# Gathered u and v rows in two rings with two requests, and the requests' new places in GpSimd's queue

## Chip, cores and metric

The kernel runs on one core of one Trainium2 chip. The metric is the device time of one execution in microseconds; that of the kernel before is the median of three runs.

## What is computed

One step of a hybrid encoder layer for 512 prompt tokens and 64 sample tokens, width 1024: an input projection, differential attention beside a gated recurrence, an output projection, cross attention, and then PEER, a layer of 16384 experts of one neuron each. Only PEER matters here. Each token scores two sets of 128 keys for each of 8 heads, takes the best 16 pairs of each head, and so has 128 experts with gates:

```python
e = (take_along_axis(i1, ci // 16) * 128 + take_along_axis(i2, ci % 16))
g = softmax(ts)
ue = u_tab[e]                      # (tokens, 8, 16, 1024)
ve = v_tab[e]
act = gelu(einsum('td,thkd->thk', xt, ue))
out = einsum('thk,thkd->td', g * act, ve)
```

## The kernel before

The five token tiles (four of 128 prompt tokens, one of 64 sample tokens) go through PEER in two ways. Tiles 0 to 2 (384 tokens) are computed **densely**: all 16384 experts for all tokens, in 128 splits of 128 experts, with the gates spread out in a matrix. Tiles 3 and 4 are **gathered**: for every token the rows of u and v of its own experts are fetched from memory by an indirect DMA, 128 rows a step. One row of the table `uv` is u's row and v's row side by side, 8 KB. There are 192 steps: 64 (`EARLY_STEPS`) for the sample tile, whose 128 experts a token are folded on two halves of the partitions, and 128 for tile 3.

A gathered step s is three pieces of work. GpSimd issues the gather into one of four places of `ring`. VectorE's `dot(s)` (L1882) multiplies u's half with the token's row and sums; ScalarE's `coefficient(s)` (L1440, L1446) applies gelu and the gate; VectorE's `accumulate(s)` (L1890) adds v's half times the coefficient to the result. VectorE does dot(s) and then accumulate(s - 2), `LAG = 2`. A gather waits until accumulate of the step whose place it takes is done.

The **split stage** is the loop over the 128 splits n on TensorE. `up(n)` multiplies the split's u weights with the tokens, 24 matmuls (L903), each weight in a high and a low part: `high(n)` is ScalarE's, `low(n)` (L496) GpSimd's, and the weights lie in four places, so that high(n) waits until `up(n - 4)` is done. ScalarE's gelu follows each split. From split 54 on, 48 placing groups g stand between the halves of the splits (`c_tokens`, L927): they multiply 0/1 matrices `hot1`, `hot2` that VectorE makes with three operations a group (L2036, L2038, L2040), to write the dense gates matrix, which goes to memory as `c_scratch`. Group g stands after half split `hot_place(g)`; group 0 after half split 108, group 47 after 250, mostly three apart. `hot_of_step(s) = s * 48 // 64` says behind which group's `hot` operations VectorE does step s, so the groups have one, one and two steps by turns. Two `hot` buffers let VectorE be one group ahead. GpSimd's queue holds low(n) and, between them, the early gathers:

```python
while RING <= issued < EARLY_STEPS and hot_place(hot_of_step(issued - LAG)) // 2 + 4 <= n:
    gather(issued)
    issued += 1
```

ScalarE does the coefficients of group g - 1 when it comes to group g's place, ahead of its copies of the matrix.

The **down stage** is a loop over 128 blocks q: SyncE loads v's weights (`vraw`, 512 KB), the gelu results (`ge`, 192 KB) and every fourth time the gates (`cg`, 768 KB); VectorE multiplies the two (`gf`, L2052); TensorE does 12 matmuls (L951). With each q VectorE does one gathered step of tile 3, in the order gf, dot, accumulate. GpSimd's queue holds nothing but the gathers there. The end is the norm and the store of the result.

Of the kernel before, what the change touches and what calls it, by code (L numbers as in the profile page):

```python
# [24 lines left out]
P = 128  # L25
D = 1024
# [60 lines left out]
def hot_of_step(s):  # L87

    return s * HOTS // EARLY_STEPS
# [83 lines left out]
def encoder_layer(nc: bass.Bass, block, a: dict, o: dict):  # L173
# [139 lines left out]
    r = Region(after_xn)  # L313
    ring = r.put("ring", [P, RING, 2 * D])
    dots = r.put("dots", [P, STEPS])
# [44 lines left out]
    def bank(b, n=BANK, rows=P):  # L360
# [18 lines left out]
    ve_step = S("ve_step")  # L379
    names = """const_in gain_in gain_used memx_in x_in ssq_clear ssq_ready var_ready std_ready xn_ready acth_done  # L380
        out_done lamp_in sp_neg sp_exp sp_one sp_ln lam_sums lam_exp lam_ready conv_done gate_ready m_ready
# [5 lines left out]
        dot_ready acted_ready coef_ready acc_done gates_ready tile3_ready fold_ready folded  # L387
        x2_in y_ready taken_up ss_in iota_copied yg4_copied""".split()
    (const_in, gain_in, gain_used, memx_in, x_in, ssq_clear, ssq_ready, var_ready, std_ready, xn_ready, acth_done,
     out_done, lamp_in, sp_neg, sp_exp, sp_one, sp_ln, lam_sums, lam_exp, lam_ready, conv_done, gate_ready, m_ready,  # L390
# [5 lines left out]
     dot_ready, acted_ready, coef_ready, acc_done, gates_ready, tile3_ready, fold_ready, folded,  # L396
     x2_in, y_ready, taken_up, ss_in, iota_copied, yg4_copied) = [S(name) for name in names]
    ck_in = [S(f"ck_in{j}") for j in range(2)]
# [10 lines left out]
    v_in = [S(f"v_in{j}") for j in range(V_RING)]  # L409
    gather_in = [S(f"gather_in{j}") for j in range(RING)]  # L410
    ss_store = [S(f"ss_store{j}") for j in range(2)]
# [60 lines left out]
    @block.gpsimd  # L472
    def _(pool):
        with pool.Fori(0, PRE_CHUNKS // 2) as i:
            for s in range(4):
                w = raw[:, s % 2, :]
                hi = wH[:, s].rearrange("p k n -> p (k n)")
                lo = wL[:, s].rearrange("p k n -> p (k n)")

                pool.wait_ge(raw_in[s % 2], i * 32 + 16 * (s // 2 + 1))  # L480
                pool.wait_ge(w_free, i * 4 + (s // 2 * 2 + 2))

                pool.sem_inc(taken_up, 1)
                cuts = (slice(0, PIECE // 2), slice(PIECE // 2, PIECE))
                for cut in cuts:
                    pool.tensor_scalar(hi[:, cut], w[:, cut], 1.0, 1.0, ALU.mult, ALU.mult).then_inc(high_done, 1)  # L486
                for c, cut in enumerate(cuts):

                    pool.wait_ge(high_done, i * 8 + (2 * s + c + 1))
                    pool.tensor_tensor(lo[:, cut], w[:, cut], hi[:, cut].bitcast(F32), ALU.subtract)\  # L490
                        .then_inc(w_ready, 1)

        def low(n):
            pool.wait_ge(hi_done, n + 1)
            u = n % U_RING
            pool.tensor_tensor(uL[:, u].rearrange("p k n -> p (k n)"), uraw[:, u, :],  # L496
                               uH[:, u].rearrange("p k n -> p (k n)").bitcast(F32), ALU.subtract).then_inc(lo_done, 1)

        def gather(s):
            if s >= RING:  # L500
                pool.wait_ge(acc_done, s - RING + 1)
            if s == STEPS4:
                pool.wait_ge(tile3_ready, 1)
            pool.indirect_dma_start(out=ring[:, s % RING, :], out_offset=None, in_=a["uv"],  # L504
                                    in_offset=bass.IndirectOffsetOnAxis(ap=place_of[:, s:s + 1], axis=0))\
                .then_inc(gather_in[s % RING], 16)

        def two_halves(out, of):

            for half in range(2):  # L510
                pool.dma_start(out[half * NS_TOK:(half + 1) * NS_TOK, 0:STEPS4],
                               of[0:NS_TOK, half * STEPS4:(half + 1) * STEPS4]).then_inc(picks_in, 16)

        issued = 0
        for n in range(NKEYS):
            low(n)
            if n == PICKS_AT:
                pool.wait_ge(picks_ready, 1)
                two_halves(place_of, eu)
            if n == PICKS_AT + 1:  # L520

                pool.wait_ge(ssb_ready, N_PQ * TILES)
                pool.wait_ge(picks_in, 32)
                for s in range(RING):
                    gather(s)
                issued = RING
            if n == GATES_AT:
                pool.wait_ge(gates_ready, 1)
                two_halves(gates_of, chosen[:, DENSE, 2, :])
            while RING <= issued < EARLY_STEPS and hot_place(hot_of_step(issued - LAG)) // 2 + 4 <= n:  # L530
                gather(issued)
                issued += 1
        for s in range(issued, STEPS):
            gather(s)

# [434 lines left out]
    def _(act):  # L970
# [443 lines left out]
        def copy_choices():  # L1414

            act.wait_ge(chT_ready, DENSE)
            act.wait_ge(iota_in, 16)
            act.activation(iota_ps, iota[:, :], ACT.Copy).then_inc(iota_copied, 1)
            for i in range(DENSE):
                act.activation(chosenT[:, :, i * P:(i + 1) * P],  # L1420
                               ps[:, i * BANK:i * BANK + 2 * P].rearrange("p (s t) -> p s t", s=2),
                               ACT.Copy).then_inc(chT_copied, 1)
# [77 lines left out]
    def _(ve):  # L1500
# [375 lines left out]
        def dot(s):  # L1876
            ve.wait_ge(gather_in[s % RING], 16 * (s // RING + 1))
            if s == 0:
                ve.wait_ge(rows_in, 16)
            x_at = 0 if s < STEPS4 else 1  # L1880
            row = ring[:, s % RING, 0:D]
            ve.scalar_tensor_tensor(row, row, 1.0, xn[:, x_at, :], ALU.mult, ALU.mult, accum_out=dots[:, s:s + 1])\  # L1882
              .then_inc(dot_ready, 1)

        def accumulate(s):
            ve.wait_ge(coef_ready, s + 1)
            if s:
                ve.wait_ge(acc_done, s)
            y = yg4 if s < STEPS4 else yg[:, 1, :]
            ve.scalar_tensor_tensor(y, ring[:, s % RING, D:2 * D], coef[:, s:s + 1], y, ALU.mult, ALU.add)\  # L1890
              .then_inc(acc_done, 1)
# [133 lines left out]
        ve.wait_ge(chT_copied, DENSE)  # L2025
        ve.wait_ge(iota_copied, 1)
        for g in range(HOTS):
# [61 lines left out]
        for j, i in enumerate(LAST):  # L2089
# [12 lines left out]

INPUTS = ["wts", "wu", "wv", "uv", "ident", "x", "mem", "gains", "par", "lamp", "gsub", "ropec", "ropes", "ropen", "mask", "ckT", "cv",
          "cmkT", "cmv", "keysT", "iota"]
# [4 lines left out]
def layout(p):  # L2109
# [28 lines left out]
    for at, name in ((PAR_CB, "conv_b"), (PAR_BA, "rg_ba"), (PAR_BX, "rg_bx")):  # L2138
# [18 lines left out]
    arrays = {  # L2157
        "wts": wts, "wu": wu, "wv": wv, "uv": np.concatenate([u, v_rows], axis=1), "ident": np.eye(P, dtype=f32),
        "x": np.concatenate([p["x_prompt"][0], p["x_sample"][0]]), "mem": p["mem_prompt"][0],
# [32 lines left out]
```

## Time and profile before

| | |
|---|---|
| median of 3 runs | 2619.72 us (2613.31 to 2626.7) |
| profiled execution, its own time | 2624.7 us |
| its span | 2622.9 us |
| granted TensorE clock, mean | 0.92 |
| TensorE / VectorE / ScalarE / GpSimd busy | 89% / 57% / 25% / 35% |
| moved | 541.94 MB, 207 GB/s |
| 192 gathers, 1 MB each | median 8.2 us from issue to landing |
| share of the gathers in the chain that ended last | 20% |

A busy share is an average over stages with different limits. "PEld" rows are TensorE's weight loads, which run beside its matmuls; a matmul's end is modelled. The granted clock is a share of full speed, and a DMA share of 1 means that all 16 engines have packets under way.

### The profile page before, as it was taken

How to read it: one execution, taken by the hardware profiler on the slowest of the kernel's cores; microseconds unless marked ns; L12 is line 12 of the kernel's file. 1: busy time of each engine (PE TensorE's matmuls, PEld its weight loads, DVE VectorE, ACT ScalarE, POOL GpSimd, SP SyncE). 2: the span in 40 equal slices, each digit the busy share in tenths (PEclk: the TensorE clock that was granted, in tenths of full speed). 3: DMA queues.
4: the chain of work that ended last, by engine and by line, in shares of the span. 5: the costliest groups of instructions: out<-in, count | busy, mean ns of one | idle time of the engine just before them, and what ended most of it. 6: DMA issues, size and time to landing. Idle time of an engine off the chain costs nothing.

```text
span 2622.9 us, 29598 instructions
## 1 busy us (share of the span) xinstructions
PE 2339.0 (89%) x11005; PEld 1786.3 (68%) x11005; DVE 1487.4 (57%) x2697; ACT 667.5 (25%) x1421; POOL 927.9 (35%) x552
## 2 busy tenths in 40 slices
PE   6799999899789999999977777777789999999996
PEld 6699977655468879999977777777734444344442
DVE  2376654444632334999985656665445555555555
ACT  2244420123322312333433333333200000000001
POOL 8454554400014244266644444444311111111110
PEclk9799999855799999999988888888899999999998
DMA  6323233200133121366547677777899999999995
GB/s 233 107 97 109 94 127 113 89 16 16 48 94 137 49 95 64 107 230 177 171 125 289 244 267 272 271 279 262 301 357 367 360 358 360 340 362 355 353 365 207
DMA packets 192546, 541.94 MB, mean 207 GB/s; under 512 B 17057, under 2 KB 116194, under 8 KB 158882
## 3 DMA queue, kind: packets, MB, share of 16 engines
q1 hardware_dynamic: 113024, 243.30, 28.1%
q0 software_dynamic: 27776, 201.40, 20.1%
q10 hardware_dynamic: 51618, 95.52, 10.0%
q8 instruction: 81, 1.33, 0.2%
q14 instruction: 47, 0.39, 0.0%
HBM read 472.18 MB, written 67.67 MB: 206 GB/s over the span
## 4 chain that ended last, share of the span: by engine, by line
PE 44%; DVE 23%; DMA 22%; issue 5%; ACT 3%; POOL 3%; ACTq 1%; SPq 0%; DVEq 0%; POOLq 0%
DMA ring<-uv,place_of 20%; PE ps L578 16%; PE ps L951 7%; PE ps L903 5%; PE ps L695 4%; PE ps L927 3%; PE ps L728 3%; DVE yg L1890 2%; PE ps L557 2%; PE ps L778 2%; POOL uL L496 1%; PE ps L732 1%; DVE chosen L1965 1%; POOL wL L490 1%; DVE pickf L1964 1%
## 5 line engine op out<-in xcount | busy, mean ns | idle before, releaser
L951 PE MATMUL ps<-vraw,gf 128*128 128x512 f32 x1536 | 675.7, 601 | 42.1 <-DVE gf L2052 31.1
L951 PEld LDWEIGHTS ps<-vraw,gf 128*128 128x128 f32 x1536 | 292.7, 192 | 424.7 <-issue 367.3
L1882 DVE SCALAR_TENSOR_TENSOR ring<-ring,xn 128x1024 f32<-128x1024 f32 x192 | 249.1, 1298 | 498.1 <-DMA ring<-uv,place_of 498.0
L496 POOL TENSOR_TENSOR uL<-uraw,uH 128x1024 fp32r<-128x1024 f32 x128 | 328.6, 2571 | 344.0 <-ACT uH L1391 343.7
L504 POOL DMA_INDIRECT ring<-uv,place_of x192 | 195.4, 1018 | 657.2 <-DVE yg L1890 573.2
L903 PE MATMUL ps<-actH,uH 128*128 128x384 f32 x1024 | 351.4, 343 | 2.7 <-POOL uL L496 2.0
L486 POOL TENSOR_SCALAR wH<-raw 128x1024 fp32r<-128x1024 f32 x112 | 120.9, 1099 | 646.1 <-PE ps L578 493.3
L903 PE MATMUL ps<-actL,uH 128*128 128x384 f32 x1024 | 345.7, 338 | 0.0
L903 PE MATMUL ps<-actH,uL 128*128 128x384 f32 x1024 | 345.1, 337 | 0.0
L578 PE MATMUL ps<-actH,wH 128*128 128x288 f32 (+1 forms) x960 | 287.1, 299 | 7.0 <-DVE actL L1552 7.0
L578 PE MATMUL ps<-actH,wL 128*128 128x288 f32 (+1 forms) x960 | 285.1, 297 | 0.0
L578 PE MATMUL ps<-actL,wH 128*128 128x288 f32 (+1 forms) x960 | 284.9, 297 | 0.0
L490 POOL TENSOR_TENSOR wL<-raw,wH 128x1024 fp32r<-128x1024 f32 x112 | 283.8, 2557 | 0.0
L927 PE MATMUL ps<-hot,hot 128*128 128x128 f32 x768 | 120.9, 323 | 119.6 <-DVE hot L2040 119.6
L1440 ACT ACTIVATE acted<-dots 128x1 f32<-128x1 f32 x192 | 38.4, 200 | 680.0 <-DVE ring L1882 669.4
L927 PEld LDWEIGHTS ps<-hot,hot 128*128 128x128 f32 x768 | 115.4, 235 | 126.0 <-DVE hot L2040 126.0
L903 PEld LDWEIGHTS ps<-actH,uH 128*128 128x128 f32 x1024 | 195.9, 191 | 3.2 <-ACT ge L1406 2.3
L903 PEld LDWEIGHTS ps<-actL,uH 128*128 128x128 f32 x1024 | 195.7, 191 | 0.0
L903 PEld LDWEIGHTS ps<-actH,uL 128*128 128x128 f32 x1024 | 194.9, 190 | 0.0
L578 PEld LDWEIGHTS ps<-actH,wH 128*128 128x128 f32 x960 | 183.6, 191 | 8.2 <-DVE actL L1552 7.9
L578 PEld LDWEIGHTS ps<-actL,wH 128*128 128x128 f32 x960 | 183.4, 191 | 0.3
L578 PEld LDWEIGHTS ps<-actH,wL 128*128 128x128 f32 x960 | 183.3, 191 | 0.0
(290 smaller groups left out, 3311.4 us busy)
## 6 DMA issues: line engine op xcount, KB each, us to landing
uraw<-wu SPq DMA_DIRECT2D x128, 512.0 KB, 4.0
vraw<-wv SPq DMA_DIRECT2D x128, 512.0 KB, 6.9
raw<-wts SPq DMA_DIRECT2D x56, 1024.0 KB, 4.9
ge_scratch<-ge ACTq DMA_DIRECT2D x128, 192.0 KB, 4.2
c_scratch<-cst ACTq DMA_DIRECT2D x12, 2048.0 KB, 9.2
cg<-c_scratch SPq DMA_DIRECT2D x32, 768.0 KB, 9.8
ge<-ge_scratch SPq DMA_DIRECT2D x128, 192.0 KB, 7.2
xres<-x ACTq DMA_DIRECT2D x2, 2048.0 KB, 12.1
```

Of the source, the lines that this page charges most:

```text
L486: pool.tensor_scalar(hi[:, cut], w[:, cut], 1.0, 1.0, ALU.mult, ALU.mult).then_inc(high_done, 1)
L490: pool.tensor_tensor(lo[:, cut], w[:, cut], hi[:, cut].bitcast(F32), ALU.subtract)\
L496: pool.tensor_tensor(uL[:, u].rearrange("p k n -> p (k n)"), uraw[:, u, :], uH[:, u].rearrange("p k n -> p (k n)").bitcast(F32), ALU.subtr ...
L504: pool.indirect_dma_start(out=ring[:, s % RING, :], out_offset=None, in_=a["uv"], in_offset=bass.IndirectOffsetOnAxis(ap=place_of[:, s:s + ...
L557: mm = pe.matmul(out, lhs, rhs, start=t == 0, stop=t == len(terms) - 1)
L578: mm = pe.matmul(cols(b), lhs, rhs, start=k == 0 and t == 0, stop=k == KT - 1 and t == 2)
L695: mm = pe.matmul(cols(b), lhs, rhs, start=k == 0 and t == 0, stop=k == KT - 1 and t == 2)
L728: mm = pe.matmul(bank(b, n), qT[half, h, t], kT[half, h, 0:n], start=True, stop=False)
L903: mm = pe.matmul(bank(b, TD), lhs, rhs, start=k == 0 and w == 0, stop=k == KT - 1 and w == 2)
L927: mm = pe.matmul(ps[:, at:at + P], hot1[:, g % 2, 4 * half + t, :], hot2[:, g % 2, 4 * half + t, :], start=True, stop=True)
L951: mm = pe.matmul(bank(2 * i + half), gf[:, q % GF_RING, i * P:(i + 1) * P], vraw[:, q % V_RING, half * CHUNK:(half + 1) * CHUNK], start=q ...
L1882: ve.scalar_tensor_tensor(row, row, 1.0, xn[:, x_at, :], ALU.mult, ALU.mult, accum_out=dots[:, s:s + 1])\
```

## The change

The ring becomes two, `ring_u` and `ring_v`, of the same size together, and the table `uv` becomes two tables; each step has two requests of 128 rows of 4 KB. The request for u(s) waits for dot(s - 4), that for v(s) for accumulate(s - 4). In GpSimd's queue both stand two splits further forward (`+ 2` for `+ 4`), and u's goes by the group of step s - 4 in place of s - 2. Behind the splits, u runs up to three steps ahead of v. One wait of VectorE (`iota_copied`) goes, which stood behind a wait for later work of the same engine, and an unused semaphore.

```diff
-    ring = r.put("ring", [P, RING, 2 * D])
+    ring_u = r.put("ring_u", [P, RING, D])
+    ring_v = r.put("ring_v", [P, RING, D])
...
-        def gather(s):
+        def gather_u(s):
+
+            if s == STEPS4:
+                pool.wait_ge(tile3_ready, 1)
+            if s >= RING:
+                pool.wait_ge(dot_ready, s - RING + 1)
+            pool.indirect_dma_start(out=ring_u[:, s % RING, :], out_offset=None, in_=a["u_rows"],
+                                    in_offset=bass.IndirectOffsetOnAxis(ap=place_of[:, s:s + 1], axis=0))\
+                .then_inc(urow_in[s % RING], 16)
+
+        def gather_v(s):
+
             if s >= RING:
                 pool.wait_ge(acc_done, s - RING + 1)
-            if s == STEPS4:
-                pool.wait_ge(tile3_ready, 1)
-            pool.indirect_dma_start(out=ring[:, s % RING, :], out_offset=None, in_=a["uv"],
+            pool.indirect_dma_start(out=ring_v[:, s % RING, :], out_offset=None, in_=a["v_rows"],
                                     in_offset=bass.IndirectOffsetOnAxis(ap=place_of[:, s:s + 1], axis=0))\
-                .then_inc(gather_in[s % RING], 16)
+                .then_inc(vrow_in[s % RING], 16)
...
                 for s in range(RING):
-                    gather(s)
-                issued = RING
+                    gather_u(s)
+                    gather_v(s)
+                u_next = v_next = RING
...
-            while RING <= issued < EARLY_STEPS and hot_place(hot_of_step(issued - LAG)) // 2 + 4 <= n:
-                gather(issued)
-                issued += 1
-        for s in range(issued, STEPS):
-            gather(s)
+            while RING <= u_next < EARLY_STEPS and hot_place(hot_of_step(u_next - RING)) // 2 + 2 <= n:
+                gather_u(u_next)
+                u_next += 1
+            while RING <= v_next < EARLY_STEPS and hot_place(hot_of_step(v_next - LAG)) // 2 + 2 <= n:
+                gather_v(v_next)
+                v_next += 1
+        while v_next < STEPS:
+            if u_next < min(STEPS, v_next + LAG + 1):
+                gather_u(u_next)
+                u_next += 1
+            else:
+                gather_v(v_next)
+                v_next += 1
...
-            ve.wait_ge(gather_in[s % RING], 16 * (s // RING + 1))
+            ve.wait_ge(urow_in[s % RING], 16 * (s // RING + 1))
...
             ve.wait_ge(coef_ready, s + 1)
+            ve.wait_ge(vrow_in[s % RING], 16 * (s // RING + 1))
...
-        ve.wait_ge(iota_copied, 1)
```

GpSimd's queue around the first early requests, before: `uL` rows are low(n), and the row with x43 ends at low(59); `ring` rows are gathers, the first of them that of step 4.

```order
L496 TENSOR_TENSOR uL<-uraw,uH 128x1024 [waits hi_done] x43
L504 DMA ring<-uv,place_of 128x2048 [waits acc_done]
L496 TENSOR_TENSOR uL<-uraw,uH 128x1024 [waits hi_done] x2
L504 DMA ring<-uv,place_of 128x2048 [waits acc_done]
L496 TENSOR_TENSOR uL<-uraw,uH 128x1024 [waits hi_done]
L504 DMA ring<-uv,place_of 128x2048 [waits acc_done] x2
L496 TENSOR_TENSOR uL<-uraw,uH 128x1024 [waits hi_done] x2
L504 DMA ring<-uv,place_of 128x2048 [waits acc_done]
```

And after the change; the row with x40 ends at low(56).

```order
L498 TENSOR_TENSOR uL<-uraw,uH 128x1024 [waits hi_done] x40
L507 DMA ring_u<-u_rows,place_of 128x1024 [waits dot_ready] x2
L498 TENSOR_TENSOR uL<-uraw,uH 128x1024 [waits hi_done]
L507 DMA ring_u<-u_rows,place_of 128x1024 [waits dot_ready]
L515 DMA ring_v<-v_rows,place_of 128x1024 [waits acc_done]
L498 TENSOR_TENSOR uL<-uraw,uH 128x1024 [waits hi_done] x2
L507 DMA ring_u<-u_rows,place_of 128x1024 [waits dot_ready]
L515 DMA ring_v<-v_rows,place_of 128x1024 [waits acc_done]
L498 TENSOR_TENSOR uL<-uraw,uH 128x1024 [waits hi_done]
```

The first request of the split stage moved from behind low(59) to behind low(56) and is now two, for u of steps 4 and 5; v of step 4 follows behind low(57), and each step takes two requests between the low parts.

The same queue where the splits end, before: the gather of step 64 and the 127 behind it.

```order
L496 TENSOR_TENSOR uL<-uraw,uH 128x1024 [waits hi_done] x2
L504 DMA ring<-uv,place_of 128x2048 [waits acc_done] x2
L496 TENSOR_TENSOR uL<-uraw,uH 128x1024 [waits hi_done]
L504 DMA ring<-uv,place_of 128x2048 [waits tile3_ready,acc_done]
L504 DMA ring<-uv,place_of 128x2048 [waits acc_done] x127
```

After:

```order
L498 TENSOR_TENSOR uL<-uraw,uH 128x1024 [waits hi_done] x2
L515 DMA ring_v<-v_rows,place_of 128x1024 [waits acc_done] x2
L498 TENSOR_TENSOR uL<-uraw,uH 128x1024 [waits hi_done] x3
L507 DMA ring_u<-u_rows,place_of 128x1024 [waits dot_ready,tile3_ready]
L507 DMA ring_u<-u_rows,place_of 128x1024 [waits dot_ready] x2
L515 DMA ring_v<-v_rows,place_of 128x1024 [waits acc_done]
L507 DMA ring_u<-u_rows,place_of 128x1024 [waits dot_ready]
L515 DMA ring_v<-v_rows,place_of 128x1024 [waits acc_done]
L507 DMA ring_u<-u_rows,place_of 128x1024 [waits dot_ready]
```

Where one kind of request stood, u and v now alternate, u three steps ahead, each with a wait of its own.

## Rows read from the trace of the kernel before

**Rows 1.** Busy time by stage: us, then each engine, PEclk, DMA share, GB/s
```profile
1348.00:1874.00 526.00, 420.45 (x2484) 414.36 (x2485) 331.23 (x336) 191.57 (x366) 239.77 (x133) 0.89 0.71 259
1874.00:1893.00 19.00, 8.64 (x50) 8.32 (x49) 2.99 (x4) 3.49 (x8) 1.74 (x2) 0.86 1.02 382
1893.00:2600.00 707.00, 675.22 (x1536) 292.70 (x1536) 370.58 (x510) 64.14 (x256) 124.28 (x124) 0.98 0.98 352
```

**Rows 2.** Waits of the split stage: us in total, times, longest
```profile
DVE ring L1882 <- DMA ring<-uv,place_of: 187.9, 34, 12.3
...
PEld ps L927 <- DVE hot L2040: 126.0, 20, 14.9
...
DVE ps L1890 <- ACT coef L1446: 4.4, 1, 4.4
```

**Rows 3.** Chain that ended last, from 1400: start, us, what
```profile
1404.62 1.78 PE ps L927 x16
1406.40 6.24 PE ps L903 x36
...
1435.57 2.05 PE ps L927 x16
...
1459.09 3.78 PE ps L927 x16
```

**Rows 4.** All placing weight loads of L927: count, first and last start
```profile
L927 PEld LDWEIGHTS ps<-hot,hot x768: 186/192/338, 1348.5 to 1871.9; 128*128 128x128 f32 x192
```

**Rows 5.** VectorE in order of time, one group of one step
```profile
1389.83 1.22 DVE L2036 TENSOR_TENSOR hot<-ps,chosenT 128x1024 f32<-128x1024 f32 x1
...
1393.35 1.25 DVE L1882 SCALAR_TENSOR_TENSOR ring<-ring,xn 128x1024 f32<-128x1024 f32 x1
...
1395.72 1.21 DVE L2036 TENSOR_TENSOR hot<-ps,chosenT 128x1024 f32<-128x1024 f32 x1
```

**Rows 6.** Gathers of the split stage: issue on GpSimd, landing
```profile
L504 POOL DMA_INDIRECT ring<-uv,place_of x63: 932/952/1878, 1364.8 to 1873.9; - x63
...
DMA to landing us min/median/max: 5.4/8.2/14.4
```

**Rows 7.** ScalarE in order of time, gelu and the coefficients behind it
```profile
1420.71 0.49 ACT L1406 ACTIVATE ge<-ps 128x384 f32<-128x384 f32 x1 [1.86 <-PE ps L903]
...
1421.61 0.20 ACT L1440 ACTIVATE acted<-dots 128x1 f32<-128x1 f32 x1 [0.40 <-ACT ge L1406]
1421.84 0.29 ACT L1446 ACTIVATE coef<-acted,gates_of 128x1 f32<-128x1 f32 x1
1422.04 0.19 ACT L1440 ACTIVATE acted<-dots 128x1 f32<-128x1 f32 x1
1422.26 0.29 ACT L1446 ACTIVATE coef<-acted,gates_of 128x1 f32<-128x1 f32 x1
```

**Rows 8.** Waits of the down stage
```profile
DVE ring L1882 <- DMA ring<-uv,place_of: 310.1, 117, 7.4
...
PE ps L951 <- DVE gf L2052: 31.1, 19, 6.8
```

**Rows 9.** Chain that ended last: the down stage's longest stretch without a wait
```profile
2533.31 67.22 PE ps L951 x156
```

**Rows 10.** DMA queues of the down stage: packets, MB, share of 16 engines
```profile
q0 software_dynamic: 17881, 130.11, 48.5%
q1 hardware_dynamic: 84625, 115.85, 47.8%
```

**Rows 11.** DMA at 1150 to 1340: queue, and issues with median landing
```profile
q1 hardware_dynamic: 6531, 23.76, 44.4%
...
uraw<-wu SPq DMA_DIRECT2D x45, 512.0 KB, 3.9
```

**Rows 12.** The same at 100 to 400
```profile
q1 hardware_dynamic: 2880, 20.97, 21.0%
...
raw<-wts SPq DMA_DIRECT2D x20, 1024.0 KB, 4.8
```

More of the change, by code:

```diff
@@ L379, in encoder_layer @@
     ve_step = S("ve_step")
-    names = """const_in gain_in gain_used memx_in x_in ssq_clear ssq_ready var_ready std_ready xn_ready acth_done
+    names = """const_in gain_in memx_in x_in ssq_clear ssq_ready var_ready std_ready xn_ready acth_done
         out_done lamp_in sp_neg sp_exp sp_one sp_ln lam_sums lam_exp lam_ready conv_done gate_ready m_ready
@@ L387, in encoder_layer @@
         dot_ready acted_ready coef_ready acc_done gates_ready tile3_ready fold_ready folded
-        x2_in y_ready taken_up ss_in iota_copied yg4_copied""".split()
-    (const_in, gain_in, gain_used, memx_in, x_in, ssq_clear, ssq_ready, var_ready, std_ready, xn_ready, acth_done,
+        x2_in y_ready taken_up ss_in yg4_copied""".split()
+    (const_in, gain_in, memx_in, x_in, ssq_clear, ssq_ready, var_ready, std_ready, xn_ready, acth_done,
      out_done, lamp_in, sp_neg, sp_exp, sp_one, sp_ln, lam_sums, lam_exp, lam_ready, conv_done, gate_ready, m_ready,
@@ L396, in encoder_layer @@
      dot_ready, acted_ready, coef_ready, acc_done, gates_ready, tile3_ready, fold_ready, folded,
-     x2_in, y_ready, taken_up, ss_in, iota_copied, yg4_copied) = [S(name) for name in names]
+     x2_in, y_ready, taken_up, ss_in, yg4_copied) = [S(name) for name in names]
     ck_in = [S(f"ck_in{j}") for j in range(2)]
@@ L409, in encoder_layer @@
     v_in = [S(f"v_in{j}") for j in range(V_RING)]
-    gather_in = [S(f"gather_in{j}") for j in range(RING)]
+    urow_in = [S(f"urow_in{j}") for j in range(RING)]
+    vrow_in = [S(f"vrow_in{j}") for j in range(RING)]
     ss_store = [S(f"ss_store{j}") for j in range(2)]
@@ L512, in two_halves @@
                                of[0:NS_TOK, half * STEPS4:(half + 1) * STEPS4]).then_inc(picks_in, 16)
-        issued = 0
+        u_next = v_next = 0
         for n in range(NKEYS):
@@ L1417, in copy_choices @@
             act.wait_ge(iota_in, 16)
-            act.activation(iota_ps, iota[:, :], ACT.Copy).then_inc(iota_copied, 1)
+            act.activation(iota_ps, iota[:, :], ACT.Copy)
             for i in range(DENSE):
@@ L1880, in dot @@
             x_at = 0 if s < STEPS4 else 1
-            row = ring[:, s % RING, 0:D]
+            row = ring_u[:, s % RING, :]
             ve.scalar_tensor_tensor(row, row, 1.0, xn[:, x_at, :], ALU.mult, ALU.mult, accum_out=dots[:, s:s + 1])\
@@ L1889, in accumulate @@
             y = yg4 if s < STEPS4 else yg[:, 1, :]
-            ve.scalar_tensor_tensor(y, ring[:, s % RING, D:2 * D], coef[:, s:s + 1], y, ALU.mult, ALU.add)\
+            ve.scalar_tensor_tensor(y, ring_v[:, s % RING, :], coef[:, s:s + 1], y, ALU.mult, ALU.add)\
               .then_inc(acc_done, 1)
@@ L2100, in _ @@
                                     ALU.mult, ALU.mult).then_inc(y_ready, 1)
-INPUTS = ["wts", "wu", "wv", "uv", "ident", "x", "mem", "gains", "par", "lamp", "gsub", "ropec", "ropes", "ropen", "mask", "ckT", "cv",
+INPUTS = ["wts", "wu", "wv", "u_rows", "v_rows", "ident", "x", "mem", "gains", "par", "lamp", "gsub", "ropec", "ropes", "ropen", "mask", "ckT", "cv",
           "cmkT", "cmv", "keysT", "iota"]
@@ L2157, in layout @@
     arrays = {
-        "wts": wts, "wu": wu, "wv": wv, "uv": np.concatenate([u, v_rows], axis=1), "ident": np.eye(P, dtype=f32),
+        "wts": wts, "wu": wu, "wv": wv, "u_rows": u, "v_rows": v_rows, "ident": np.eye(P, dtype=f32),
         "x": np.concatenate([p["x_prompt"][0], p["x_sample"][0]]), "mem": p["mem_prompt"][0],
```

## Prediction

> **What bounds the kernel now.** I read the busy shares by stage first [rows 1]. Two stretches matter to this change. The **split stage**, where the placing matmuls of L927 stand between those of L903, takes 526.0 us, and TensorE works 420.45 of them at a granted clock of 0.89; the **down stage** takes 707.0 us with TensorE busy for 675.22 at 0.98. The transfers differ more: share 0.71 and 259 GB/s against 0.98 and 352 GB/s.
>
> Next the waits of the split stage [rows 2]. TensorE's weight loads wait 126.0 us, 20 times, for `hot` of VectorE; the first of these (14.9) lies before 1348.5 almost wholly, so 19 waits and 111 us lie inside. VectorE for its part waits 187.9 us for the gather, 34 times. The chain [rows 3] shows what a stall costs beyond itself: 16 placing matmuls take 1.78 us between other work, 2.05 or 3.78 behind a stall (the clock was down to its 1.2 GHz level there), and 36 of L903 take 6.24.
>
> TensorE's own work follows from that. From the first to the last placing group [rows 4] lie 142 half splits, 71 splits of 24 matmuls at 6.24/36 = 0.173 us, 4.16 each, together 295.4; 48 groups at 1.78 add 85.4. That is 380.8 us of 526.0. The excess is 145: 111 of waits and some 34 of slow clock behind them.
>
> In the down stage VectorE waits even longer for the gather, 310.1 us, but TensorE only 31.1 for `gf` [rows 8]. A stretch without waits runs 156 matmuls in 67.22 us [rows 9], 5.17 for the 12 of one q, 662 us for 128; the stage takes 707, or 5.52 a q. Its transfers are at the limit by the share. So the gather's lateness binds the first stage, and the amount moved binds the second.
>
> **The change part by part.** *Earlier requests, split stage.* Let P be the split in which the placing group of step s-2 lies. The old request for step s stands behind low(P+4); low(n) can't run before TensorE begins split n-3, so the request leaves at P+1 plus a split's fraction for ScalarE and GpSimd, say P+1.8. A split with its part of the placing takes 380.8/71 = 5.36 us. The `hot` that stands behind dot s is due at P+4.5 at the latest, 2.7 splits or 14.5 us later. In that time there must pass 8.2 from issue to landing (5.4 to 14.4) [rows 6], 2.4 for dot and accumulation (twice that in a group of two steps) and 3.5 for three `hot` operations [rows 5]: 14.1 to 16.5, so up to 2 us late at the median landing and up to 8 at the longest. Measured are 111/48 = 2.3 a group.
>
> The new request for u of step s stands two splits further forward and goes by the group of step s-4, 2.3 splits earlier again: 4.3 splits, 23 us sooner. Its place is free at dot s-4, three groups (24 us) before it is used. v gains two splits (11 us) and is needed only two steps later, at the accumulation. Against a landing of 8.2, 14.4 at worst, both are in time. The cover for this is the ring's 24 us; it is gone if landings pass some 20.
>
> *What is late next.* VectorE's work in three groups is 3 x 3.52 + 4 x 2.37 = 20.0 us [rows 5] against TensorE's 3 x 8.02 = 24.1. Accumulation s-2 can need a coefficient of the group before, which ScalarE computes behind the gelu: gelu at 1420.71, second coefficient done at 1422.55 [rows 7], so 1.9 us after TensorE could begin its placing. Then 1.2 for the accumulation and 3.5 for `hot`: 6.6 of 8.02, in time by 1.4. GpSimd issues two requests a step in place of one, 64 x 0.95 us more [rows 6]; it waits in queue order for dot_ready and acc_done, and behind it stands low(P+3). That wait ends about when TensorE does split P, low(P+3) is due three splits later, so 16 us cover it. The transfers' own work is 0.71 x 526 = 373 us [rows 1], just under the 381 of TensorE: little room, and bursts will be felt. I leave 25 us for them, half a microsecond for each of 48 groups: less than a quarter of the 111 of today, as the landings that hurt are the longest only. Bounds: 0 (floor 381) and 60 (434, below). Stage: 406, gain **120**.
>
> *Earlier requests, down stage.* In flight now are at most two gathers of 1 MB, later up to four u and four v of half that. The amount is the same. At share 0.98 there are 14 us (2% of 707) that a fuller queue can win.
>
> *Twice the packets.* A gathered row of 8 KB becomes two of 4 KB. In the down stage [rows 10] q0 spends 0.485 x 707 x 16 / 17881 = 0.307 us on a packet of 7276 bytes, q1 0.478 x 707 x 16 / 84625 = 0.064 on one of 1369. A line through both gives 0.0076 us a packet beside its bytes: 128 more packets on 16 engines are 0.06 us a step, 8 us in the down stage and 4 in the split stage (hidden there if TensorE is the bound). I take the line, since it is from this stage and at this load. Bounds: nothing, and the rows of streams without gathers beside them [rows 11, 12]: 20 requests of 1 MB held the engines for 0.210 x 300 / 20 = 3.15 us each, 45 of half that size for 0.444 x 190 / 45 = 1.88, so two halves cost 0.6 more than the whole. Gain 14 less 8, less a little for a fuller queue that SyncE's loads must share: I take **0** for the down stage.
>
> The Trainium skill, "DMA: Bandwidth & Descriptors", section "Anatomy of one DMA", gives 2.0 us plus bytes/436e3 for one software request. By that (an estimate) two halves cost 2.0 us more than one whole; laid end to end over 128 steps, this would be 256 us. The trace bears out the latency (half the bytes land in 3.9 us, the whole in 4.8 [rows 11, 12]) but not the adding up: gathers that land in 8.2 us come every 5.5.
>
> *The rest*: the dropped wait for iota_copied stands behind one for the same engine's later work; nothing.
>
> **Sum.** 2624.7 - 120 - 0 = 2504.7 by the profiled execution, which lies 5 us above the median of the runs: **2500**.
>
> **The rivals.**
> *A. The down stage gains too* (0.12). If share 0.98 hides latency and not capacity, more requests in flight let it run to TensorE's 662 plus some 13 of start: 675, 32 less, 2468. For it: the 19 us between the stages moved 382 GB/s. Against: 352/0.98 = 359 GB/s, and the split stage has 259/0.71 = 365 per full share [rows 1], so both show the same ceiling. The skill's same page, section "Where 436 GB/s comes from", puts a core's half of the memory at some 358 and measured 425 with the neighbour idle; the rows agree with the first.
> *B. Half requests hold the engines longer* (0.13, and 0.04 for its far end). With x us more a step the down stage takes 128x more, and the split stage 373 + 64x + 6 once that passes 406. At q1's rate of today, 115.85/(0.478 x 707) = 343 GB/s against q0's 379 [rows 10], x is 0.29: 2500 + 37 + 0 = 2537, with some disturbance of the first stage 2543. At the 0.6 of the lone streams: 418 and +77, 2589. **The other side:** at the uraw rate of 23.76 MB/(0.444 x 190) = 281 GB/s [rows 11], x is 0.98: split stage 440 (the upper bound above), down stage +125, so 2500 + 34 + 125 = 2659, slower. It decides at x = 0.76, a gather rate of 297 GB/s. Against it: those streams were alone and paid their start each time.
> *C. ScalarE's coefficient takes the gather's place* (0.08). If the 1.4 us of room are short by 3 in two groups of three, 96 us come on the floor: 477, a gain of 49, 2571. For it: VectorE waited for it once already, 4.4 us [rows 2].
> *D. Nothing moves* (0.03): landings under a share near 1 grow with what is in flight, and VectorE waits as long as before.
>
> **How the numbers follow.** The likeliest (0.60) reaches from 2480 to 2525 (residue 5 to 50 us). Range 2450 to 2570: it takes in A, B up to 0.4 us a step, and stops at C. Some 13 us (0.5%) is what a measurement can tell here. Faster by more: 0.60 + 0.12 + 0.13 + 0.08 = 0.93; D is the same, 0.03; slower 0.04.
>
> **What would show it.** In the split stage: weight loads' wait for `hot` under 35 us, VectorE's for gathers under 50 (that for coef may rise to 30), a clock of 0.95 or more, a share of 0.9; length 400 to 430. In the down stage: 695 to 715 at a share of 0.98 or more, u and v landing in 8 us and more as before. A down stage under 685 speaks for A, over 735 for B; `hot` late with gathers in time and coef as releaser for C. The forecast fails most likely in the down stage, where one tenth of a microsecond in a step is 13 us.

## The result, and the profile after

The changed kernel takes 2473.96 us (median of four runs, 2465.09 to 2476.26) against 2621.14 for the kernel before (2613.31 to 2626.7): a ratio of 0.943, with a 95% interval of 0.940 to 0.947. The forecast of 2500 was 26 us too high: within its range of 2450 to 2570, but below the 2480 to 2525 of its likeliest case. The profiled execution took 2465.09 us, with a span of 2463.3, and is the fastest of the four.

By stage, the rows that answer to [rows 1]:

```profile
1347.00:1746.00 399.00, 389.61 (x2483) 384.68 (x2484) 392.88 (x336) 191.18 (x366) 287.95 (x196) 0.99 0.93 342
1746.00:1764.00 18.00, 8.70 (x51) 8.38 (x49) 2.25 (x3) 3.00 (x6) 1.53 (x2) 0.84 1.01 377
1764.00:2441.00 677.00, 664.72 (x1537) 293.00 (x1538) 368.31 (x512) 65.99 (x259) 311.47 (x250) 0.99 1.00 369
```

The split stage went from 526 to 399 us, the down stage from 707 to 677. These are 127 and 30 of the 159.6 us between the two profiled executions (2624.7 to 2465.1); the other 2.6 are in the stretches before, between and behind them. TensorE's clock is 0.99 in both, and the share of the transfers 0.93 and 1.00, with 342 and 369 GB/s against 259 and 352.

The waits of the split stage (us in total, times, longest), beside [rows 2]:

```profile
POOL ring_u L507 <- DVE ring_u L1902: 92.7, 59, 12.6
...
PEld ps L947 <- DVE hot L2060: 24.1, 17, 10.3
...
POOL ring_v L515 <- DVE ps L1911: 20.4, 45, 4.4
...
DVE ps L1911 <- ACT coef L1466: 4.1, 1, 4.1
```

TensorE's wait for `hot` fell from 126.0 to 24.1, VectorE's for the gather from 187.9 to nothing that is listed. The new place of waiting is GpSimd, 92.7 us for dots. And VectorE is busy for 392.88 of the 399 us, more than any other engine. The row of its dots in the split stage, by tile (shortest, median, longest in ns):

```profile
L1902 DVE SCALAR_TENSOR_TENSOR ring_u<-ring_u,xn x64: 1209/1364/5093, 1347.3 to 1742.1; 128x1024 f32<-128x1024 f32 x64
```

In the down stage:

```profile
L1902 DVE SCALAR_TENSOR_TENSOR ring_u<-ring_u,xn x128: 1209/1218/1283, 1763.5 to 2425.9; 128x1024 f32<-128x1024 f32 x128
```

A dot takes 1.22 us, but in the split stage the longest takes 5.09. What stands beside the long ones is seen in order of time. VectorE from 1377 to 1403 (start, us):

```profile
1376.01 1.28 DVE L1911 SCALAR_TENSOR_TENSOR ps<-ring_v,coef,ps 128x1024 f32<-128x1024 f32 x1
...
1380.71 4.90 DVE L1902 SCALAR_TENSOR_TENSOR ring_u<-ring_u,xn 128x1024 f32<-128x1024 f32 x1
...
1385.55 1.28 DVE L1911 SCALAR_TENSOR_TENSOR ps<-ring_v,coef,ps 128x1024 f32<-128x1024 f32 x1
...
1390.25 1.35 DVE L1902 SCALAR_TENSOR_TENSOR ring_u<-ring_u,xn 128x1024 f32<-128x1024 f32 x1
...
1396.24 3.71 DVE L1902 SCALAR_TENSOR_TENSOR ring_u<-ring_u,xn 128x1024 f32<-128x1024 f32 x1
...
1401.07 1.21 DVE L1902 SCALAR_TENSOR_TENSOR ring_u<-ring_u,xn 128x1024 f32<-128x1024 f32 x1
```

GpSimd in the same stretch, where L498 is the low part and the brackets are its idle time and what ended it:

```profile
1377.59 0.94 POOL L515 DMA_INDIRECT ring_v<-v_rows,place_of  x1 [0.30 <-DVE ps L1911]
1378.83 0.94 POOL L515 DMA_INDIRECT ring_v<-v_rows,place_of  x1 [0.30 <-issue]
1379.79 4.74 POOL L498 TENSOR_TENSOR uL<-uraw,uH 128x1024 fp32r<-128x1024 f32 x2
1385.89 0.95 POOL L507 DMA_INDIRECT ring_u<-u_rows,place_of  x1 [1.37 <-DVE ring_u L1902]
1387.15 0.94 POOL L515 DMA_INDIRECT ring_v<-v_rows,place_of  x1 [0.30 <-DVE ps L1911]
1388.11 2.40 POOL L498 TENSOR_TENSOR uL<-uraw,uH 128x1024 fp32r<-128x1024 f32 x1
```

The dot of 1380.71 starts inside the two low parts that GpSimd runs from 1379.79 for 4.74 us, and ends 1.1 us behind them, at 1385.6. The one of 1390.25 meets only the last 0.3 us of a low part and takes 1.35; the one of 1401.07 meets none and takes 1.21. So it is in the whole stage: 46 of the 64 dots take over 1.3 us, each of them begins inside a low part and ends 1.08 to 1.10 us behind the last of the low parts that run there without a pause; none of the other 18 begins inside one. The accumulations of this stage, which have one of their inputs in PSUM (`ps`), take 1.29 us at most.

In the down stage the wait of VectorE for the gather [rows 8] is gone too, and it waits for the loads instead:

```profile
DVE gf L2072 <- DMA ge<-ge_scratch: 299.5, 76, 25.5
...
PE ps L971 <- DVE gf L2072: 11.7, 2, 11.2
PE ps L971 <- DMA vraw<-wv: 9.8, 1, 9.8
```

Those 299.5 us cost little: TensorE lost 21.5 us to both of its waits, `gf` and the first load. Before, it lost 31.1 to `gf` [rows 8] and 10.7 to the first load:

```profile
PE ps L951 <- DMA vraw<-wv: 10.7, 1, 10.7
```

That is 20 of the stage's 30 us; the rest is TensorE's own work, 664.72 us at a granted clock of 0.99 for 675.22 at 0.98. The DMA queues (packets, MB, share), beside [rows 10]:

```profile
q0 software_dynamic: 36000, 131.09, 49.9%
q1 hardware_dynamic: 84481, 115.47, 48.7%
```

q0 has twice the packets, as it should, and took 0.499 of the stage for 131.09 MB: 388 GB/s, more than the 379 of before (130.11 MB in 0.485 of 707 us, [rows 10]).

### The profile page after: what moved, and what is told of

Its sections match the earlier page's. It is cut to its first block, busy times and chain, and to the rows that moved or that the text cites. A ratio compares the mean times of both kernels' runs of the same rounds, so it can differ in the third digit from the quotient of the medians.

```text
span 2463.3 us, 29790 instructions
## 1 busy us (share of the span) xinstructions
PE 2297.0 (93%) x11005; PEld 1757.1 (71%) x11005; DVE 1544.5 (63%) x2697; ACT 666.8 (27%) x1421; POOL 1166.9 (47%) x744
## 3 DMA queue, kind: packets, MB, share of 16 engines
q10 hardware_dynamic: 51618, 95.52, 10.7%
## 4 chain that ended last, share of the span: by engine, by line
PE 56%; DVE 31%; issue 5%; DMA 3%; ACT 2%; SPq 2%; POOL 1%; ACTq 0%; POOLq 0%; DVEq 0%
PE ps L971 24%; PE ps L598 17%; DVE ring_u L1902 5%; PE ps L715 5%; DVE ps L1911 3%; PE ps L748 3%; DVE hot L2058 2%; DVE hot L2056 2%; DMA ge<-ge_scratch 2%; PE ps L577 2%; PE ps L798 2%; PE ps L752 1%; SPq L447 1%; DVE pickp L1982 1%; DVE chosen L1986 1%
## 5 line engine op out<-in xcount | busy, mean ns | idle before, releaser
L971 PE MATMUL ps<-vraw,gf 128*128 128x512 f32 x1536 | 664.7, 595 | 21.6 <-DVE gf L2072 11.7
L507 POOL DMA_INDIRECT ring_u<-u_rows,place_of x192 | 235.9, 1229 | 411.6 <-DVE ring_u L1902 391.8
L498 POOL TENSOR_TENSOR uL<-uraw,uH 128x1024 fp32r<-128x1024 f32 x128 | 323.4, 2539 | 116.0 <-ACT uH L1411 114.9
L1902 DVE SCALAR_TENSOR_TENSOR ring_u<-ring_u,xn 128x1024 f32<-128x1024 f32 x192 | 312.8, 1629 | 0.0
L2072 DVE TENSOR_TENSOR gf<-ge,cg 128x384 f32<-128x384 f32 x128 | 71.8, 561 | 305.4 <-DMA ge<-ge_scratch 305.0
L515 POOL DMA_INDIRECT ring_v<-v_rows,place_of x192 | 203.9, 1062 | 71.4 <-issue 45.6
```

The costliest lines, as they stand in the source:

```text
L507: pool.indirect_dma_start(out=ring_u[:, s % RING, :], out_offset=None, in_=a["u_rows"], in_offset=bass.IndirectOffsetOnAxis(ap=place_of[:, ...
L515: pool.indirect_dma_start(out=ring_v[:, s % RING, :], out_offset=None, in_=a["v_rows"], in_offset=bass.IndirectOffsetOnAxis(ap=place_of[:, ...
L971: mm = pe.matmul(bank(2 * i + half), gf[:, q % GF_RING, i * P:(i + 1) * P], vraw[:, q % V_RING, half * CHUNK:(half + 1) * CHUNK], start=q ...
```

## Experiments

Stage lengths come from each trace, the split stage from the first placing group to the last, the down stage from the first of its matmuls to the last; a whole is the median of the runs, with its ratio to the kernel before, run on the same chip beside it. "+4" and "+2" are the splits that the queue's condition adds; "s-4" and "s-2" say by which step's group u's request goes. "Paired": behind the splits u runs no steps ahead of v.

| kernel | u, v requests | place in the splits | split stage | down stage | whole | ratio |
|---|---|---|---|---|---|---|
| before | one | +4 | 526 | 707 | 2621.1 | 1 |
| e1_two_requests | two, dot waits for both | +4 | 534 | 747 | 2672.6 | 1.020 (1.017 to 1.023) |
| e1c_u_alone | two, dot waits for u | +4 | 495 | 673 | 2561.4 | 0.978 (0.975 to 0.981) |
| e3_old_places | as changed | +4, u by s-2 | 499 | 680 | 2577.1 | 0.984 (0.980 to 0.987) |
| e2_forward_only | one | +2 | 426 | 703 | 2526.4 | 0.966 (0.962 to 0.969) |
| e4_no_lead_down | as changed, paired behind the splits | +2 | 399 | 676 | 2469.2 | 0.940 (0.937 to 0.944) |
| after_again | as changed | +2 | 399 | 678 | 2470.3 | 0.943 (0.940 to 0.945) |
| e10_plus3 | as changed | +3 | 403 | 676 | 2474.2 | 0.944 (0.942 to 0.947) |
| e12_plus4 | as changed | +4, u by s-4 | 390 | 678 | 2464.6 | 0.940 (0.938 to 0.943) |
| e13_plus4_paired | as e12, paired | +4, u by s-4 | 388 | 674 | 2463.4 | 0.940 (0.937 to 0.942) |
| e5_low_halves | as changed, low part in halves | +2 | 406 | 681 | 2467.5 | 0.940 (0.937 to 0.943) |
| e8_low_eighth | as changed, an eighth of the low part | +2 | 386 | 679 | 2455.0, one run | |
| e9_low_memset | as e8, with a memset | +2 | 386 | 680 | 2456.1, one run | |

A stage's length is from one trace a kernel. Eight traces have the changed kernel's code in the down stage; they give 676 to 681 us for it.

Theory and rivals at the start: what counts is the *lead* of a request before its use; against it, that *half requests* run better or worse by themselves, and that the *place* freed at dot is the point.

**Two requests and nothing else.** The request for u waits for acc_done as v's does, both stand at the old place, one behind the other, and the dot waits for both:

```diff
             ve.wait_ge(urow_in[s % RING], 16 * (s // RING + 1))
+            ve.wait_ge(vrow_in[s % RING], 16 * (s // RING + 1))
```

> Two rings and two half requests a step, but with everything else as before: both wait for accumulate(s-4), stand at the old places, and dot waits for u and v. Theory 'lead' (what counts is how long before its use a request is issued): split stage 526 us and down stage 707 us as in the kernel before, plus at most 12 us for the doubled packets, so 2620 to 2635 us. Rival 'size' (half requests by themselves let the transfers run faster): down stage 690 or less, whole 2605 or less. Rival 'half requests hold the engines longer' (0.6 us a step): 2690 or more.

It was slower by 2.0% (1.7 to 2.3), outside all three expectations: 2672.6 us lies between "lead" and "half requests hold the engines longer". Its stages (columns as in [rows 1]):

```profile
1354.00:1888.00 534.00, 425.80 (x2486) 419.65 (x2487) 352.07 (x336) 191.60 (x367) 297.54 (x194) 0.88 0.72 256
1907.00:2654.00 747.00, 683.12 (x1536) 291.20 (x1536) 368.59 (x509) 63.17 (x254) 243.16 (x248) 0.98 0.94 333
```

Its gathers in the down stage, with the median from issue to landing, and their queue:

```profile
ring_u<-u_rows,place_of POOLq DMA_INDIRECT x124, 6.8
ring_v<-v_rows,place_of POOLq DMA_INDIRECT x124, 7.5
...
q0 software_dynamic: 35781, 130.26, 47.9%
```

The down stage took 40 us more, 0.31 a step. The DMA engines were not held: the share is 0.94, lower than before. The loss is in the round from a freed place to the next arrival, which takes two steps, as dot(s) uses what was requested behind accumulate(s - 4). v's half lands 7.5 us after the start of its issue, which is 1.3 us after the start of u's (1.01 for u's issue, 0.30 to the next): together 8.8 against 8.2 for the whole before. With 0.3 us from the freed place to the issue and 2.4 for dot and accumulation the round is, by this estimate from medians, 10.9 us before and 11.5 here; measured are 11.05 (707/64) and 11.67 (747/64). Half the request lands only 0.7 us sooner than the whole, and the second issue costs more than that.

**Dot waits for u alone.** The same without that added wait.

> As the kernel with two requests and nothing else, but dot waits for u alone, v only at the accumulation. Lead: half the data stand ahead of dot, so it starts some 1 to 2 us sooner; split stage 470 to 510, down stage 690 to 700, whole 2550 to 2595 us. Rival 'place' (u's place freed at dot is the point): no gain without it, 2615 us or more.

The whole takes 111 us less than the kernel above. By the two traces it is 118, 74 of it in the down stage and 39 in the split stage. Its stages:

```profile
1351.00:1846.00 495.00, 418.55 (x2485) 411.70 (x2486) 343.55 (x336) 191.00 (x366) 298.75 (x194) 0.92 0.77 275
1865.00:2538.00 673.00, 665.83 (x1538) 293.87 (x1538) 372.54 (x510) 65.61 (x257) 246.02 (x248) 0.99 1.01 370
```

Its waits in the down stage, TensorE's and VectorE's:

```profile
DVE ring_u L1901 <- DMA ring_u<-u_rows,place_of: 243.8, 113, 5.2
...
PE ps L970 <- DMA vraw<-wv: 10.3, 1, 10.3
...
PE ps L970 <- DVE gf L2071: 7.2, 1, 7.2
```

So the down stage's whole gain (673 us, the shortest of all) is there once v may come two steps later: VectorE still waits 243.8 us for u, TensorE next to nothing for VectorE. The whole (2561.4) and the split stage (495) came within the forecast of "lead"; the down stage is 17 us under its 690 to 700. The "place" theory fell: u's place was still held until the accumulation.

**One request, two splits forward.** In the kernel before, `hot_place(...) // 2 + 2 <= n` for `+ 4`.

> The kernel before with its one request moved two splits further forward (+2 for +4) and nothing else. Lead: the request then waits mostly for accumulate(s-4) itself, 8.2 us of landing against two steps of about 12 us, so most of the split stage's waits go: 430 to 460 us; the down stage has no such places and stays at 707; whole 2535 to 2560 us. Rival 'place': the request can't leave before accumulate(s-4), so the stage stays above 500 us and the whole above 2590.

100 of the split stage's 127 us come from this line alone; the down stage, where the line has no part, stayed at 703. Both the stage (426) and the whole (2526.4) came out a little below the forecast of "lead", far below that of "place". The waits of its split stage:

```profile
POOL ring L504 <- DVE ps L1890: 202.4, 61, 25.8
...
DVE ring L1882 <- DMA ring<-uv,place_of: 53.8, 20, 7.7
PEld ps L927 <- DVE hot L2040: 44.0, 14, 14.8
```

GpSimd now waits 202.4 us with the request in hand, so what its request waits for is the place of the ring, free only at the accumulation; VectorE still waits 53.8 us for the gather, and the stage is 27 us longer than in the changed kernel. That the place is why is argued from these waits.

**Rings as changed, old places.**

```diff
+            while RING <= u_next < EARLY_STEPS and hot_place(hot_of_step(u_next - LAG)) // 2 + 4 <= n:
+                gather_u(u_next)
+                gather_v(u_next)
```

> The changed kernel with both requests at the old places of the split stage (+4, group of step s-2), the down stage as changed. Lead: down stage 677 us as in the changed kernel; split stage between before and after, 450 to 500, because u needs half the data; whole 2520 to 2570 us. If the places were of no account, 2474 us.

Both of its stages came out as said, 499 and 680; the whole, 2577.1, is 7 us above the 2570 of the forecast. Against e1c_u_alone it shows what u's freed place and, in the down stage, three steps of lead bring: no gain, in either stage (499 against 495, 680 against 673).

**No lead of u behind the splits.** `u_next < min(STEPS, v_next + 1)` for `v_next + LAG + 1`.

> The changed kernel, but behind the splits u no longer runs up to three steps ahead of v: GpSimd issues u(s), v(s), u(s+1). The kernel in which only dot's wait for v had gone already had a down stage of 673 us by its trace, so if two steps more for v are what counts, the down stage is 670 to 680 here too and the whole 2465 to 2480 us. If the early u (its place free at dot) carries part of the down stage's gain, 685 or more and 2485 or more.

676 us and 2469.2, within the first of the two expectations, and no slower than the changed kernel. VectorE waits 62.8 us for u here, which costs TensorE nothing that shows.

**The low part in halves.** Two tensor_tensor of 512 columns for one of 1024.

> The changed kernel with GpSimd's low part of each split done in two operations of 512 columns. Theory 'lock' (a dot, which reads two tensors of SBUF, stands still while a GpSimd operation that reads SBUF runs): if dot can step in between two GpSimd operations, the dots' 1.6 us mean of the split stage falls to 1.5 and less and the stage from 398 to 385 to 392 us, whole 2460 to 2468. If GpSimd's next operation takes the port before dot does (as two low parts in a row did, 4.9 us), no change, 2470 to 2478.

2467.5 us (0.940, 0.937 to 0.943), the split stage 406 by its trace, and the dots' sum in one same window of 393 us 163.07 against 156.29 in the changed kernel. A dot didn't come in between two GpSimd operations: one that began at 1374.77 took 5.17 us, through four halves that ran from 1373.83 to 1378.84. The whole fell where the first theory had it (2460 to 2468), and yet the dots, and the split stage of 406 us, are as the second has them. So this kernel is inconclusive on the time, and clear on the order of access.

**An eighth of the low part, and a memset for the rest.** From split 54 on; the low weights left out are part of the computation.

```diff
-            pool.tensor_tensor(uL[:, u].rearrange("p k n -> p (k n)"), uraw[:, u, :],
+            cut = P if n >= HOT_AT else D
+            pool.tensor_tensor(uL[:, u].rearrange("p k n -> p (k n)")[:, 0:cut], uraw[:, u, 0:cut],
```

> The changed kernel, from split 54 on with an eighth of the low part (128 of 1024 columns; the rest of the low weights is left out, so the time is that of less work on GpSimd). Lock: no dot over 1.7 us, the dots' sum in the split stage falls from 157 us to 80, and the stage goes down to TensorE's 381 to 386 us, whole about 2450. If the dots are long because of the transfers' writes into SBUF, they stay long and the stage stays at 398.

> As the one before, with the left-out 896 columns filled by a GpSimd memset, which writes SBUF and reads none. If the dots' standing still comes from GpSimd's reading, they stay at 1.2 us and the stage at 381 to 386; if any GpSimd operation on SBUF does it, dots of 2 us and more are there again and the stage is 388 or more.

They ran at 2455 and 2456 us (one run each), with the split stage at 386 in both. The dots of the first:

```profile
L1904 DVE SCALAR_TENSOR_TENSOR ring_u<-ring_u,xn x64: 1215/1218/1254, 1348.0 to 1728.3; 128x1024 f32<-128x1024 f32 x64
```

And of the second, with the memset:

```profile
L1906 DVE SCALAR_TENSOR_TENSOR ring_u<-ring_u,xn x64: 1215/1219/1348, 1347.1 to 1727.5; 128x1024 f32<-128x1024 f32 x64
```

GpSimd's memset in the second, 71 times 0.86 us in that stage:

```profile
L500 POOL MEMSET uL<- 128x896 f32 x71 | 61.1, 861 | 18.3 <-ACT uH L1415 18.2
```

With most of GpSimd's reading gone no dot takes over 1.35 us, and the stage is 13 us shorter; the transfers, which moved 355 GB/s there, are not the cause. That GpSimd's writes are not the cause either rests on less than the 61 us of memsets: only ten of the 64 dots met one, and nine of these memsets began inside the dot. Each of the ten dots took 1.22 us, and each of these memsets 0.85 or 0.86: neither waited for the other. So the long dots come from GpSimd's operations that read SBUF. The Trainium skill states this: "SBUF — State Buffer", section "Who interferes with whom", says that a VectorE instruction with two SBUF inputs contends with a GpSimd instruction that reads SBUF and not with one that only writes it, and that the second to start waits for the whole of the first. Dot reads `ring_u` and `xn`; these rows agree, 1.22 us without and up to 5.09 with. They show one thing more: the dot of 1380.71 let both of two low parts pass that followed each other, and those of e5_low_halves up to four.

**Other places.** Both one split later (`+ 3`); or `+ 4` with u by the group of s - 4; and this with the paired order.

> The changed kernel with both requests one split later (+3 for +2). Theory 'ring of waits' (GpSimd, at the request, waits for the dot just done, then does its low parts, and these hold up the next dot): one split later the dot waited for is long done, the low parts come when ScalarE releases them, fewer of them meet a dot, and the dots' sum in the split stage falls from 157 us to 100 to 130; stage 385 to 393, whole 2458 to 2468. Rival 'lead': one split less of lead (5.4 us) brings waits for the gather back, stage 405 or more, whole 2480 or more.

> The changed kernel with both at +4 as in the kernel before, but u still by the group of step s-4 (so 2.3 splits ahead of the old place), v by that of step s-2 (the old place). v is needed only at the accumulation two steps later, so its old place is early enough. Ring of waits: stage 383 to 390 us, whole 2455 to 2465. Lead: if v's two splits were needed, waits for ring_v appear, stage 410 or more.

> The one before with the down stage's order u(s), v(s) in place of u three steps ahead: down stage 673 to 677 by the two kernels that had it, so 0 to 5 us less than the one before, the best of all: 2452 to 2464 us.

And the changed kernel beside them:

> The changed kernel once more, beside the three that follow: 2465 to 2480 us, split stage 398 us, down stage 677.

`+ 3` was a miss: 403 us and 2474.2. The dots' sum fell to 144 us only, not to 100 to 130, and TensorE's weight loads waited 29.7 us for `hot`, more than in the changed kernel. `+ 4` with u by s - 4 came out as said (2464.63, 2463.99 to 2467.77). Paired it has the lowest median, 2463.42 us (2462.82 to 2465.67), by less than the runs differ among themselves; both are under the 2470.32 (2468.41 to 2476.03) of the changed kernel run beside them. The paired kernel's waits in the split stage:

```profile
DVE ps L1911 <- ACT coef L1466: 28.4, 15, 4.5
...
PEld ps L947 <- DVE hot L2060: 15.6, 4, 12.3
```

GpSimd waits for dots for 0.3 us in all there, dots take 116 us in place of 157, and the coefficient (28.4 us) is VectorE's longest wait.

## Why the prediction was right

**The whole.** The direction and the range held. The medians are 147 us apart where 120 were forecast, and 2474 lies below the likeliest case (0.60) and beside the 2468 of rival A, which had 0.12. So it was the width of the range, drawn to take in A, that made room for the result, and not its central sum. The sign that the prediction had named for A, a down stage under 685 us, came true too.

**What bounds the stages.** That the gather's lateness bound the split stage is shown by one moved line that took 100 us (e2_forward_only). The floor of 381 us held within 5: with short dots the stage takes 386.

**Split stage: 406 forecast, 399 measured, gain 120 against 127.** The size was nearly right, in part by luck: the 25 us of residue were set down to bursts of transfers that make landings late, and no wait for a gather is listed, with landings up to 14.0. (Its upper bound stands as 434 in one place and as 440 in another; 381 and 60 are 441.) Most of the 18 us over the floor are dots held up by low parts, as 13 of them went when the low parts were cut (e8_low_eighth): the dots take 157.5 us in this stage where 64 x 1.22 = 78 would do, and VectorE, which I had at 20.0 of 24.1 us for three groups, is busy for 392.88/16 = 24.6. The chain that ended last goes through it (start, us), a round of three groups from one of these rows to the next, 76.2 us for three:

```profile
1376.08 1.20 DVE ps L1911
...
1402.29 1.20 DVE ps L1911
...
1426.12 1.20 DVE ps L1911
...
1452.29 1.20 DVE ps L1911
```

In the trace before, eight of the 64 dots already took 2.1 to 3.4 us, and I took the one dot of [rows 5] without looking at the longest of its kind in that stage:

```profile
L1882 DVE SCALAR_TENSOR_TENSOR ring<-ring,xn x64: 1217/1226/3423, 1348.4 to 1869.8; 128x1024 f32<-128x1024 f32 x64
```

**GpSimd's waits in queue order** were costed at nothing, with 16 us of cover. Low parts were in time, as said. What I missed is that these waits tie GpSimd to VectorE: it leaves its wait when a dot is done, issues its requests, and starts the low parts just as the next dot comes. With the requests placed later the tie is gone, and the stage is 388 to 390 us. That the tie is the cause is argued, from the waits (92.7 us for dots against 0.9 and 0.3), the order in time and a count. The 71 low parts of 2.4 us fill 43% of the changed kernel's stage, so by chance, an estimate, some 27 of 64 dots would begin inside one. The dots over 1.3 us are 46 there, and 27 and 24 in e12_plus4 and e13_plus4_paired. `+ 3`, which still has 54.2 us of the wait and 39 such dots, gained nothing.

**Down stage: 0 forecast, 30 measured.** This step failed: "At share 0.98 there are 14 us (2% of 707) that a fuller queue can win." With it fell the reading against rival A that 359 and 365 GB/s per full share are one ceiling, and the agreement that the prediction saw there with the lower of the two rates it quoted. The stage moved 369 at 1.00 and 370 at 1.01. A share near 1 said that the engines always had packets under way, not that they could move no more. What bound the stage, by the estimate beside e1_two_requests, was the round of the ring, two steps long: the requests waited for accumulate(s - 4), and the dot for the whole row. Rival A gave 675 us for this stage; 677 were measured. Its mechanism needs a correction: not the many requests in flight but that v may come two steps later, since e1_two_requests and e1c_u_alone issue their requests by the same rule, and differ by 74 us in the one wait for v. TensorE is now the bound there, with 664.72 of 677 us busy, so no run shows how much more the engines could move.

**Twice the packets.** The line through the two queues gave 0.06 us a step. Two requests by themselves cost 0.31. The sum of the round in e1_two_requests puts that down to the second issue on GpSimd, with no run that has the issue alone. The packets' own time is small: by q0's rows two packets of 4 KB take 0.320 us in e1_two_requests and 0.300 in the changed kernel, where one of 8 KB took 0.307. So the term was put at the wrong resource. In the changed kernel it is hidden, as VectorE has no wait for a gather there, and rival B didn't come: q0's rate rose.

**The coefficient (rival C)** is a wait of VectorE of 4.1 us in the changed kernel, of 30.0 and 28.4 in e12_plus4 and e13_plus4_paired, and of 66.3 in e8_low_eighth. It costs almost nothing: TensorE's weight loads wait 3.3 us for `hot` in e13_plus4_paired beyond the one wait of 12.3, and in e8_low_eighth, where the stage is the shortest, once, for 6.4 us. The 96 us of rival C didn't come; the 1.4 us of room itself was not measured.

**The sum.** 127 + 30 + 2.6 = 159.6 against 120, so 2465 for the profiled execution in place of 2505. That execution lies 9 us under the median of its four, while the one before lay 4 above that of its own; 12 us of the 159.6 come from there, and the medians give 147.

## What to carry to other kernels

Split a transfer where its parts are needed at different times, and let each consumer wait for its part alone: in the down stage the split itself cost 40 us here and the wait taken off v gave 74 back. A share of the DMA engines near 1 is no proof of a limit on the amount; compare the round trip of a ring (steps in flight, landing, issue) with the measured step before calling a stage bound by transfers. And when a wait moves to an engine's queue, look at what that engine starts right behind the wait, and whom it disturbs.

## What the runs showed that I had not expected

GpSimd's issue of a gather stands still beside VectorE's operations too. In the down stage of the changed kernel the median issue for u takes 1.74 us, for v 0.94. VectorE in order of time, the accumulation (L1911), which has both inputs in SBUF there, and a dot:

```profile
2005.96 1.28 DVE L1911 SCALAR_TENSOR_TENSOR yg<-ring_v,coef,yg 128x1024 f32<-128x1024 f32 x1
...
2010.32 1.28 DVE L1911 SCALAR_TENSOR_TENSOR yg<-ring_v,coef,yg 128x1024 f32<-128x1024 f32 x1
...
2011.98 1.22 DVE L1902 SCALAR_TENSOR_TENSOR ring_u<-ring_u,xn 128x1024 f32<-128x1024 f32 x1
```

GpSimd in the same stretch:

```profile
2006.31 1.74 POOL L507 DMA_INDIRECT ring_u<-u_rows,place_of  x1 [6.54 <-DVE ring_u L1902]
2008.36 0.94 POOL L515 DMA_INDIRECT ring_v<-v_rows,place_of  x1 [0.30 <-issue]
2010.67 1.74 POOL L507 DMA_INDIRECT ring_u<-u_rows,place_of  x1 [1.37 <-DVE ring_u L1902]
2012.71 1.31 POOL L515 DMA_INDIRECT ring_v<-v_rows,place_of  x1 [0.30 <-issue]
```

The issue of 2006.31 starts 0.35 us into the accumulation and ends 0.81 behind its end (2007.24), at 2008.05; the next, for v, starts with VectorE idle and takes 0.94. The issue of 2010.67 starts inside an accumulation again and ends 0.81 behind it, and that of 2012.71, inside a dot, ends 0.82 behind the dot.

The whole stage is like these rows. 125 of its 250 issues begin inside an accumulation, a dot or a `gf` (all with two inputs in SBUF), over 0.1 us behind its start and over 0.13 us ahead of its end; all 125 end 0.80 to 0.82 us behind the end of that operation. Of the other 125, all but one take 0.93 or 0.94. In the split stage 120 of the 126 issues begin in the same way inside an operation with one input in PSUM, such as the one at 1385.89 inside the accumulation of 1385.55, and these take 0.93 to 0.97; the three that begin inside a dot take 1.38 to 1.74. No experiment was made for this, so that the second input in SBUF is the cause is argued from these counts.
